# Expert loop ordered by weight tile, an early fixed expert, biases by shuffle, new filler places in the recurrent heads

## The reference

```python
def hgrn2_chunk_scan(q, k, v, log_f, s0):      # for each head, each direction
    def step(state, inp):
        cum = jnp.cumsum(gc, axis=2)
        o_inter = jnp.einsum('bhtk,bhkv->bhtv', qc * jnp.exp(cum), state)
        ...
        att = jnp.einsum('bhtk,bhtsk,bhsk->bhts', qc, decay, kc)
        o_intra = jnp.einsum('bhts,bhsv->bhtv', att, vc)
        ...

def moe_ffn(h, w_router, b_router, w_gate_up, b_gate_up, w_down, b_down):
    logits = (t @ w_router + b_router).astype(jnp.float32)
    top_val, top_idx = lax.top_k(logits, TOP_K)
    probs = jax.nn.softmax(top_val, axis=-1)
    ...
    def expert_block(args):
        xb, e = args
        gu = xb @ w_gate_up[e] + b_gate_up[e]
        x_glu = jnp.minimum(gu[:, 0::2], SWIGLU_LIMIT)
        x_lin = jnp.clip(gu[:, 1::2], -SWIGLU_LIMIT, SWIGLU_LIMIT)
        act = x_glu * jax.nn.sigmoid(SWIGLU_ALPHA * x_glu) * (x_lin + 1)
        return act @ w_down[e] + b_down[e]
```

## Time and profile before

| | us |
|---|---|
| median of 3 runs | 3326.22 |
| lowest, highest | 3324.42, 3329.95 |
| the profiled execution | 3331.52 |
| its span | 3329.8 |
| PE busy | 3017.5 |
| DVE busy | 952.9 |
| ACT busy | 681.7 |
| mean granted clock of PE, share of full | 0.941 |

### The profile page before, as it was taken

How to read it: one execution, slowest core, us unless ns; L and a number is a source line. 1 busy time by engine, 2 the same in 40 slices (tenths; PEclk the granted TensorE clock), 3 DMA queues, 4 the chain that set the end, 5 groups by cost and what they waited for, 6 DMA issues and landing times.

```text
span 3329.8 us, 46098 instructions
## 1 busy us (share of the span) xinstructions
PE 3017.5 (91%) x19817; PEld 1561.9 (47%) x19817; DVE 952.9 (29%) x1975; ACT 681.7 (20%) x1408; POOL 188.9 (6%) x180
## 2 busy tenths in 40 slices
PE   6899989999899999889989877699899999999995
PEld 2555434444345666666556655433333333333343
DVE  2244220000122221555445455321121212111223
ACT  0133110000012333344443332111010111111102
POOL 0000000000000000211111111100000000000001
PEclk8999889999999999999999988799899999998997
DMA  3134312211211113311110110598999979999696
GB/s 152 51 124 177 118 51 76 76 63 51 103 36 32 34 45 114 114 45 45 45 45 20 45 39 2 191 418 337 418 373 383 418 310 418 397 380 391 266 391 238
DMA packets 120062, 585.13 MB, mean 176 GB/s; under 512 B 10196, under 2 KB 25716, under 8 KB 73012
## 3 DMA queue, kind: packets, MB, share of 16 engines
q1 hardware_dynamic: 95904, 536.14, 40.6%
q10 hardware_dynamic: 17652, 24.25, 2.0%
q0 software_dynamic: 6304, 21.80, 1.8%
HBM read 551.58 MB, written 30.57 MB: 175 GB/s over the span
## 4 chain that ended last, share of the span: by engine, by line
PE 79%; DMA 9%; DVE 6%; ACT 3%; another core or an unknown queue 1%; issue 1%; ACTq 0%; SPq 0%; POOL 0%; DVEq 0%; POOLq 0%
PE product_banks L874 37%; PE product_banks L1284 14%; PE product_banks L1306 8%; DMA space<-in_wgu 6%; PE score_banks L1178 3%; DMA x<-in_wgu 2%; PE out_bank L1037 1%; PE score_banks L974 1%; PE out_bank L996 1%; PE product_banks L1203 1%; PE turn_bank L947 1%; PE product_banks L861 1%; PE out_bank L957 1%; DMA space<-in_wdn 1%
## 5 line engine op out<-in xcount | busy, mean ns | idle before, releaser
L874 PE MATMUL product_banks<-space 128*128 128x512 f32 (+2 forms) x3888 | 1383.4, 508 | 39.0 <-ACT space L1414 19.4
L874 PEld LDWEIGHTS product_banks<-space 128*128 128x128 f32 x3888 | 686.1, 196 | 614.0 <-issue 547.4
L1284 PE MATMUL product_banks<-space 128*32 128x512 f32 x4864 | 583.8, 614 | 55.3 <-DMA space<-in_wgu 52.4
L1284 PEld LDWEIGHTS product_banks<-space 128*32 128x32 f32 x4864 | 141.7, 111 | 377.0 <-issue 270.4
L1306 PE MATMUL product_banks<-space,rstd 128*32 128x256 f32 x5024 | 301.9, 393 | 1.9 <-DMA space<-in_wdn 0.8
L2085 DVE TENSOR_TENSOR sq<-product_banks,cst 128x512 f32<-128x512 f32 x85 | 58.8, 692 | 748.5 <-PE product_banks L1284 748.5
L1414 ACT ACTIVATE space<-product_banks 128x512 f32<-128x512 f32 (+1 forms) x226 | 109.9, 522 | 767.0 <-PE product_banks L874 745.3
L1306 PEld LDWEIGHTS product_banks<-space,rstd 128*32 128x32 f32 x5024 | 168.4, 114 | 163.1 <-issue 72.1
L787 POOL TENSOR_TENSOR space<-space 128x512 f32<-128x512 f32 x112 | 132.6, 1198 | 999.9 <-ACT space L1566 901.8
L1178 PE MATMUL score_banks<-space 128*128 128x64 f32 x896 | 125.4, 288 | 27.3 <-issue 21.1
L1178 PEld LDWEIGHTS score_banks<-space 128*128 128x128 f32 x896 | 123.8, 211 | 42.2 <-issue 38.3
(11 more groups left out here) (319 smaller groups left out, 2478.4 us busy)
## 6 DMA issues: line engine op xcount, KB each, us to landing
space<-in_wgu SPq DMA_DIRECT2D x232, 1024.0 KB, 21.3
space<-in_wdn SPq DMA_DIRECT2D x116, 1024.0 KB, 22.4
space<-in_wt SPq DMA_DIRECT2D x104, 1024.0 KB, 5.1
x<-in_wgu SPq DMA_DIRECT2D x24, 1024.0 KB, 23.6
y_rows<-zeros ACTq DMA_DIRECT2D x2, 6400.0 KB, 29.3
x<-in_wdn SPq DMA_DIRECT2D x12, 1024.0 KB, 23.2
y_rows<-zeros ACTq DMA_DIRECT2D x84, 128.0 KB
space<-in_wt SPq DMA_DIRECT2D x13, 512.0 KB, 4.5
```

Of the source, the lines that this page charges most:

```text
L874: ins = nc.tensor.matmul(bank[0:rows, at:at + cols], lhsT, rhs, start=(i == 0), stop=(i == len(mm) - 1))
L1284: ins = nc.tensor.matmul(bank[ROWS * g:ROWS * g + ROWS, :], xT_[:, k, :], w[:, 512 * g:512 * g + 512], start=(k == 0), stop=(k == DC - 1))
```

## The change

Six edits in one.

1. ACT evacuates the first product of in1 before the norm of the memory rows, and the first four before sine and cosine.
2. `HEAD_SLOTS` holds product counts instead of weights. There is a new place for fillers between the state terms of d=1 and the wait for the states. The wait for the states of d=0 moves behind the transposes of d=1. Behind the outputs stand two products of the set of the head after the next, after a wait for the evacuations of the next head's set. `MIX_SLOTS` gives head 7 its 28 products in three places.
3. The expert loop goes by chunks of up to three blocks of one expert. A tile is used by all blocks of a chunk before the next tile. `down` of chunk i-2 stands before `up` of chunk i, whose middle has the transposes of chunk i-1. Three accumulation banks serve up.
4. Biases are loaded by two small DMAs a place into one partition in 32, and a DVE shuffle spreads them. PE's bias products, ACT's copies and DVE's selector go.
5. One expert (number 16, 42 tokens, two blocks) has place 0 fixed. Its first ten tiles are issued after the last head, two more after eight products of the output projection (`s_o2`), without the table. The order of slots in the ring changes with it; tile 18 is the one that waits for the turned inputs.
6. `BLOCKS_AT` has another order; the total stays 84 blocks and 31 places.

```diff
-HEAD_SLOTS = [7, 1, 5, 1] + [1] * 14 + [2]
+HEAD_SLOTS = [21, 1, 20, 3, 13] + [6, 6, 6, 5, 5, 5, 5] + [2, 2, 2, 2, 2, 3, 3]
+MIX_SLOTS = [18, 0, 10]
...
-BLOCKS_AT = [2, 3, 2, 5, 1, 3, 2, 4, 2, 2, 4, 2, 2, 3, 2, 5, 2, 3, 2, 3, 2, 3, 3, 2, 3, 2, 6, 1, 4, 2, 2]
+BLOCKS_AT = [2, 1, 3, 3, 3, 2, 2, 6, 1, 3, 3, 2, 2, 5, 2, 3, 2, 2, 5, 2, 2, 4, 2, 3, 2, 4, 2, 3, 2, 4, 2]
...
             norm_root("pre_mix")
+            evacuate_to(stages["in1"][0] + 1)
             norm_root("mem")
+            evacuate_to(stages["in1"][0] + 4)
             act.wait_ge(s_ang, 1)
...
                     pe.wait_ge(s_ktc, 2 * n + d + 1)
+                    if d:
+                        pe.wait_ge(s_st, 2 * n + 1)
                     for j in range(5):
...
                     ins.then_inc(s_ds, 1)
-                    pe.wait_ge(s_st, 2 * n + d + 1)
+                fill(4)
+                pe.wait_ge(s_st, 2 * n + 2)
...
-                fill(18)
+                if n < 7:
+                    pe.wait_ge(s_evac, stages[f"hg{n + 1}"][1])
+                    fillers[n + 1].lead(2)
                 norm(f"head{n}")
...
+                for t in range(MT):
+                    if t == EARLY_TILES:
+                        sp.wait_ge(s_o2, DC)
+                    sp.dma_start(tile_slot(t, t), early_source(t)).then_inc(s_w[t], 16)
...
+                    if q == 0:
+                        sp.wait_ge(s_bzero, 1)
+                    elif q > 1:
+                        sp.wait_ge(s_bc, q - 1)
+                    if q != 1:
+                        load_bias(e, raw_bias[q % 2], s_brow[q % 2])
+                    for t in range(MT if q else 0):
...
+                for k in range(DC):
+                    if i and k == DC // 2:
+                        turn_chunk(i - 1)
+                    if c.first:
+                        pe.wait_ge(*tile_landed(c.q, k))
+                    for b in range(c.at, c.at + c.n):
+                        if k == 0 and b >= CHUNK:
+                            pe.wait_ge(s_u, b - CHUNK + 1)
+                        ins = up_step(UP[b % CHUNK], block_inputs(b), k, slots[(MT * c.q + k) % NS])
...
+            for i in range(N_CHUNKS):
+                for n in TURNS_BEFORE[i]:
+                    turn_inputs(n)
+                if i >= 2:
+                    down_chunk(i - 2)
+                up_chunk(i)
+            down_chunk(N_CHUNKS - 2)
+            turn_chunk(N_CHUNKS - 1)
+            down_chunk(N_CHUNKS - 1)
...
+            def spread_bias(source, to):
+                V.stream_shuffle(to, source, [0] * ROWS).then_inc(s_bc, 1)
```

More of the change, by code:

```diff
@@ L1 @@
+from collections import namedtuple
 import numpy as np
@@ L273, in build @@
         xTb = [A.take(DC * P, DC) for _ in range(2)]
-        actb = [A.take(256) for _ in range(2)]
+        actb = [A.take(256) for _ in range(CHUNK)]
+        yb_third = A.take(256)
         attention_tables = cst[:, CONST_AT["band"]:CONST_AT["tri"]]
@@ new lines, in down_chunk @@
+            def down_chunk(i):
+                c = CHUNKS[i]
+                pe.wait_ge(s_atc, i + 1)
+                if c.at:
+                    pe.wait_ge(s_y, c.at)
+                for d in range(4):
+                    if c.first:
+                        pe.wait_ge(*tile_landed(c.q, DC + d))
+                    for b in range(c.n):
+                        ins = down_step(DN[b], aT[b], d, v3(slots[(MT * c.q + DC + d) % NS], 2), b != 1, b != 0 or c.n == 1)
+                        if d == 3:
+                            ins.then_inc(s_dn, 1)
+                    if d < 3 and c.last:
+                        ins.then_inc(s_free, 1)
```

385 lines of the change are left out of this document (200 added, 185 removed).

## The result

| | before | after |
|---|---|---|
| median | 3328.09 us | 3232.47 us |
| profiled execution, span | 3329.8 us | 3231.8 us |
| granted clock, mean | 0.941 | 0.949 |

The ratio of after to before is 0.9715, with an interval of 0.9698 to 0.9731: 96 us of 3328 are gone. The forecast was 3192, with a range of 3150 to 3238 for 8 in 10; the narrower range of 3175 to 3208, to which it gave half its chances, was missed. The direction was right, and so were the mechanisms of in1, the heads and the loop; 40 of the 136 us that the sum promised did not come, 9 of them because head 7 gained next to nothing.

The account below looks back on a forecast made before the run. PE was taken to bound the heads and the tile stream to end last in the expert loop. Against the profiled 3331.5 us, -16 - 54 - 10 - 56 = -136 gave 3195.5, taken as 3192 (3175 to 3208; 8 in 10: 3150 to 3238).

Parts of the forecast that it names:

- in1: Start of the kernel: ACT evacuating before it waits for the angles removes PE's 13.1 us idle time; -16 us.
- Heads 0 to 6: Refilled waits cut each head from 93.8 to 85.7 us; over 6.6 heads, -54 us.
- The range's end of -20: Heads 0 to 6: smallest gain, -20 us, if ACT's level chain sets the pace.
- Head 7: Last head: products fill the 13.3 and 7.0 us gaps and bare levels shrink a little; -10 us.
- The loop: Expert loop: tile stream starts earlier and runs without gaps at 2.85 us a tile; -56 us.
- The bound of -34: Expert loop's smallest gain: only the twelve early tiles, 12 x 2.85, count and the 43 us idle time stays in another form.
- rival 4: Expert loop gains only its twelve early tiles: 3213 us; chance 0.15.
- The slack of PE: Expert loop: PE needs some 943 us against the tile stream's 1009, a slack of 66.
- rival 1: PE's clock falls in the expert loop: 3362 us at 0.80; chance 0.05 slower, 0.04 for a clock in between.
- Rival 2: Expert loop's tile stream beats 2.85 us a tile and PE ends last: 3132 to 3140 us; chance 0.10.
- Rival 3: Heads gain only 20 us because a chain through ACT and DVE sets a level's pace: 3226 us; chance 0.14.
- The signs that I had named: Trace checks on gaps, head spacing, tile stream, DMA share, waits and clock; wrong signs included slot waits over 10 us.

Follow-up runs that it names:

- the two runs with other slots: Kernel after with HEAD_SLOTS moving filler products from a head's levels to earlier waits: 3209.97 us; with more moved, 3196.34 us.
- single blocks: Kernel after with chunks of one block instead of up to three in the expert loop: 3254.90 us.
- doubled transposes: Kernel after with each transpose of gated values in the expert loop issued twice: 3237.16 us.
- even order: Kernel after with another order of the 31 places, putting places of many blocks between small ones later on: 3232.60 us.
- head 7's spread products: Kernel after with head 7's 28 products placed as before, one beside nearly each level, the last two left out: 3231.49 us.

## Why the prediction was right, and where it was not

**in1** was right in cause and size: 16.8 for 16, and 15 when undone.

**Heads 0 to 6** gained 37.4 for 54. The step that failed is the sum of what stays. I had 3.4 us of gaps and no lower clock. The trace after has 2.19 + 0.59 + 0.46 + 0.65 + 0.82 = 4.7 us of gaps, the 0.46 and 0.65 inside the level chain, where I had put none. And the lower clock didn't go: three of heads 1 to 5 have one stretch of 3.4 us at it, behind a 2.19 gap, and take 88.4 or 88.5 us instead of 87.2. PE's work, 82.3 by my sum, is 82.4 in the heads of 87.2 us; with the gaps and 0.9 for the clock that is the measured mean of 88.0. The last of the intervals gained less than the others: from kd to kd the five full ones had a mean of 93.7 us before and 87.9 after, while the one that ends at head 7 went from 90.5 to 88.3. My 6.6 heads counted 0.6 of it like the others. The range's end of -20 was for a level chain through ACT and DVE that sets the pace. It cost only the 1.1 us above; late levels of 2.61 us were PE's work, and the two runs with other slots, which took products out of them, show it. The view that would have told me is PE's timeline of late levels with two wide products (0.84 + 2 x 0.88): I had the work right but never asked whether products would be better placed elsewhere.

**Head 7** gained nothing for 10. The 13.3 us gap became 4.76 and the 7.0 became 3.05, so the products did move into the gaps; the step that failed is the price of a bare level. I had put it between 1.2 and 1.75 us. From the first level to the fifteenth it took 25.8 us after, 1.84 a level, against 28.6 with the products between them, so the levels gave back 2.8 us. I noted that bare levels do not raise the clock and did not price it: the clock was at its lower level for 41 us from 1963 on, and the fifteenth level, the outputs and the norm took 3.3 us more than before. The run with the products beside the levels and the one with the whole head part undone say the same: with either placement the time of head 7 is the same.

**The loop** gained 42.9 for 56. The sum let tile 18 land at 2171 and the last fixed tile 354 x 2.85 = 1009 us later. I set it beside the landings of tile 18 and of the last fixed tile in both traces:

| | before | after | gained | forecast |
|---|---|---|---|---|
| first up product to tile 18's landing | 23.3 | 9.2 | 14 | 17 |
| to the last fixed tile's landing, 353 tiles | 1047.8 | 1017.2 | 31 | 39 |
| to the end | 93.6 | 95.4 | -2 | 0 |

The direction of each term was right. The mis-sized one is the rate: 2.88 us a tile and not 2.85, where it was 2.97 before. The 2.85 came from a stretch of 60 tiles at a DMA share of 0.98, and the new stream as a whole is at 0.96. By that share the stream stood for about 75 us of its 1065 before (0.93) and for about 41 of 1017 after (0.96); I had counted 43 us as idle and let all of them go. Tile 18 came 3 us later than forecast, behind the clearing of the bias row, whose memsets I had put at nothing. The runs fit the first two rows: without early tiles the loop is 13 or 14 us longer, with single blocks 22 to 29. The bound of -34 and rival 4 took the twelve early tiles for 34 us. They left out that the stream stands once 18 tiles are in, and that without the early ones it would have most of the 18 by the time PE starts.

The slack of PE was right as far as it was tried: 18 us of added work cost 1 to 5. That the bias products leave PE was given nothing directly, and stays untested.

**The rivals.** The clock did not fall in the loop as a whole (rival 1): 0.97 at 955 us busy of 1040, in spite of some 80 us of waits for tiles, in pieces of half a microsecond to seven. Up products of the kernel after, 2100 to 3150 (busy, mean ns, idle before):

```profile
L1337 PE MATMUL product_banks<-space 128*32 128x512 f32 x4912 | 572.1, 614 | 85.3 <-issue 52.4 <-DMA space<-in_wgu 24.0 <-ACT space L1676 8.8
```

The 52.4 us without a releaser are 13 waits ahead of the first tile of a place; in ten of them that tile's semaphore moved 0.09 us before PE went on, and in the other three the trace has no record of it. Of the windows of 50 us from 2115 to 3115, the three that hold the waits of 7 us have the lowest clock, 0.87 to 0.90. The rule of the Trainium skill's page "TensorE: Matmul & The Clock Gate", section "HAM oscillation — how this bites in real kernels", is for products that are shorter than the wait for the next tile, and that then start at the lower clock. The loop as a whole doesn't meet it, with PE busy 92% of the time. Rival 2, a faster stream, did not come: PE waits for tiles to the end. Rival 3 gave the heads 20 us; they gained 37, and its chain cost 1.1 us a head. Rival 4 gave the loop 21 less than the sum, 35, not far from 43, with the reason upside down: the early tiles are the small part.

**The signs that I had named.** No gap near 73 us: right. Heads 85.7 apart: 88.0. No issue gap before the levels, 2 us before kd: right. Head 7's first gap under 3: 4.76. The second pass of tiles starting at 2086: 2112, by what the heads and head 7 lack. DMA share near 0.98: 0.96. PE's waits for tiles of 60 us or more at a clock above 0.93: right, some 80 at 0.97, though the profile puts only 30 of them down to a DMA. Two of the signs of being wrong also came: SP waited for a slot for over 10 us at a time (up to 19.2), and the first three levels of a head were 2.85, 2.34 and 2.23 us apart. Neither meant what I had tied to it, as the loop's 43 us and the heads' 37 show; of those three levels only one has a wait in it, 0.46 us.

## What to carry to other kernels

Prefetching into a ring is worth only what the stream would still be behind when the consumer starts; once the ring is full, what counts is how early the consumer frees slots, so put items first that need nothing else that is late. Where items differ in how long they hold their buffers, release them buffer by buffer (the loop by tiles and not by blocks): that was worth 22 to 29 us, about twice the prefetch. Look also at what small work a new scheme puts ahead of the stream: here the clearing of a bias row was the last thing that a tile waited for. And after filler work has been placed, read where the filled stretches are the engine's own work: moving filler from there to the waits that are left gave 36 us by nothing but a list of numbers.

## What the runs showed of the hardware that was not expected

- PE's clock stayed at its lower level, 1.2 of 2.4 GHz (granted 0.50), for 58 us on end in head 7 with doubled levels, and in 47 of them PE was busy all the time with products of 128x64. One wide product a level, as before the change, had 0.87 in the same levels:

```profile
2028.00:2053.00 25.00, 25.00 (x129) 18.76 (x128) 17.29 (x36) 7.39 (x20) 9.14 (x8) 0.87 0.00 1
```

  The Trainium skill's page "TensorE: Matmul & The Clock Gate", section "Part 1: The HAM clock gate", ties the clock to how busy PE has been; a busy share of 1.00 in the profile was not enough here.
- At the loop's start ACT and DVE stood for about 8 us behind finished PE work. PE's products for ACT ended at 2101.07, its last one for DVE at 2101.27, and:

```profile
2105.50 0.97 POOL L854 DMA_INDIRECT token_of_row<-space  x1 [0.30 <-issue]
2108.91 0.60 ACT L1675 ACTIVATE space<-score_banks 128x512 f32<-128x512 f32 x1 [39.33 <-remote]
2108.95 0.26 DVE L2134 TENSOR_SCALAR space<-turn_bank 128x96 f32<-128x96 f32 x1 [17.28 <-remote]
```

  The kernel before and the first four runs (heads undone, no early tiles, doubled transposes, even order) have it too: there ACT starts 6.3 to 8.3 us behind the products that it waits for. In the other eight traces it starts 0.03 or 0.04 us behind them. In all six stalled traces ACT starts 2.4 to 2.8 us after the last of POOL's 16 indirect DMAs (L854) ends, and in the other eight 4.6 to 5.5 us before that end. Nothing in the edits accounts for the difference, and its cause stays open. It doesn't simply add to the time either: from head 7's first kd transposes to the end the kernel after takes 1287.6 us with the stall, and four traces without it and with the same code in that stretch (the longer slot lists, in1 undone) or nearly so (head 7's spread products) take 1280.7 to 1287.3.
